# A two-block transformer kernel: five instead of six recombined pairs in each up-projection, with its row copies and turning sums spread out

## Chip, cores and metric

The kernel runs on one core of a Trainium2 chip. The metric is the device time of one execution in microseconds (us), less is better. TensorE (PE in the profile) multiplies, VectorE (DVE) and ScalarE (ACT) work on tiles in SBUF and on the PE's sums in PSUM, SyncE (SP) and GpSimd (POOL) issue DMAs. Each engine takes its own instructions in order, and semaphores order the engines against each other.

## The reference

The whole model is two blocks one after the other on a 512 x 1024 float32 activation. The part that matters here is the feed-forward of the first block, which runs twice (once a layer):

```
def conv_ffn(xn, w_up, conv_w, conv_b, w_down):
    h = causal_dwconv(xn @ w_up, conv_w) + conv_b
    gate, val = h[..., :FFN_DIM], h[..., FFN_DIM:]
    return (jax.nn.silu(gate) * val) @ w_down
...
for layer in range(DEPTH):                       # DEPTH = 2
    h = h + (gated_deltanet or chunk_attention)
    h = h + conv_ffn(rmsnorm(h, f_norm[layer]), f_w_up[layer], f_conv[layer], f_conv_b[layer], f_w_down[layer])
```

`w_up` is 1024 x 5632 (FFN_DIM is 2816, a gate half and a value half), and the convolution runs over three neighbouring rows of the sequence.

## The kernel before

**Precision.** Each float32 operand is used as two float32r parts, a rounded one (hi) and the rest (lo). A product is three matmuls: w_hi x_hi, w_hi x_lo and w_lo x_hi. A raw weight tile is loaded by SP into `wraw`, ACT copies it to hi (a cast, L1634 or L1952) and DVE makes lo by subtraction (L2351 or L2758), both in `wsplit`.

**The up-projection** (`ffn`, one function on each engine) works through KF = 22 pairs f = 0 to 21, each a gate tile and a value tile of 128 columns. Activations lie as 8 tiles of 128 x 512 (`xhi`, `xlo`). Pairs 0 and 1 are four tiles j = 0 to 3 in a loop of their own. Of the pairs from UP_FIRST = 2 on there are two kinds:

- A plain pair (`up_tile`, twice): 8 x 3 matmuls 128x512 for the gate into bank `pa`, the same for the value into bank `pb`, 48 in all.
- A block pair (`up_block`, for f in UP_BLOCKS): the 2 x 2 recombination of Strassen and Winograd, seven products in place of eight. It has seven forms (a11, s2, a12, s1, s3, s4, a22) of 4 x 3 matmuls 128x256, 84 in all. DVE builds s2 and s4 from weights (`sum_low`, `sum_high`), two POOL DMAs that add in flight build s1 and s3 out of the three quarter tiles of `load_bases`, and four forms (s2, s1, s3, a22) need turned activations xb1 to xb4.

**The turned activations** are made once a layer. ACT writes eight unsplit rows `x_raw` (L1998, step "raw"), DVE makes the four sums `turn` (L2777) into `xb_raw`, ACT casts them (`turn_hi`, L1977), and DVE subtracts (`turn_low`, L2781), in place over `xb_raw`. The matmuls of form s2 wait for `turn_low` 1, s1 for 0, s3 for 2 and a22 for 3.

**Weights roll** through a ring of six places in `wsplit`; a plain tile takes two places, a form one. The table UNITS_AFTER says which units are cast after which one is used: for plain pairs it is the unit three tiles on. `casts_after` on ACT and `lows_after` on DVE walk that table. The units after "old2" and "old3" are those that may overwrite the splits of tiles j = 2 and j = 3: the gate of pair 2, and the value of pair 2 with the gate of pair 3. Raw weights have one buffer for gates and one for values: SP issues `load_gate(f)` when `low` of the previous gate is done, then `load_value(f)`, then `load_bases(f+2)` where f + 2 is a block pair.

**Behind the matmuls.** For each pair DVE multiplies the bank by `rstd` (L2867, L2882, step "ev", which also frees the bank), ACT applies the newest tap (`newest`, L1968), DVE the two older ones (`conv`, L2763 and L2765), ACT the silu, DVE the product (L2896, step "hid"), and for f < UP_KEPT = 6 ACT and DVE split the row (`row_hi` L1983, `row_low` L2787). All steps of DVE and ACT are counted by two semaphores; `up_counts` lists them in the order of issue, and that list must agree with the engine code. So where a step stands in `up_counts` is where it stands in the engine's queue.

Before, block pairs are 4, 7, 10, 13, 16 and 19. All eight `x_raw` rows are written after tile j = 1, ahead of the casts for "old2". Sums 0 and 1 come between the gate and the value of pair 2, sums 2 and 3 after its value; their lows in the same places of pair 3.

Of the kernel before, what the change touches and what calls it, by code (L numbers as in the profile page):

```python
# [15 lines left out]
ALU = mybir.AluOpType  # L16
ACT = mybir.ActivationFunctionType
# [80 lines left out]


UP_FIRST = 2  # L100
UP_BLOCKS = (4, 7, 10, 13, 16, 19)
UP_FORMS = ("a11", "s2", "a12", "s1", "s3", "s4", "a22")
UP_KEPT = 6
UP_LOADS = (KF - UP_FIRST, KF - UP_FIRST - len(UP_BLOCKS), 3 * len(UP_BLOCKS), 0)
UP_SUMS = 32 * len(UP_BLOCKS)

# [36 lines left out]
def up_counts():  # L143

    def lows(q):
        return [("low", u) for u in UNITS_AFTER[q]]

    def his(q):
        return [("hi", u) for u in UNITS_AFTER[q]]

    dve = lows("old2") + lows("old3")
    act = [("raw", k) for k in range(KD)] + his("old2") + his("old3")
    for f in range(UP_FIRST, KF):
        if f in UP_BLOCKS:
            dve += lows((f, "a11")) + [("u", f)] + lows((f, "s2")) + [("c11", f)] + lows((f, "a12")) + [("w", f)] + lows((f, "s1"))
            dve += [("c22", f), ("v", f)] + lows((f, "s3")) + [("c12", f), ("ev", f, 0)] + lows((f, "s4")) + [("c21", f), ("ev", f, 1)]
            dve += lows((f, "a22")) + [("tap", f, 0), ("conv", f, 0), ("tap", f, 1), ("conv", f, 1), ("hid", f)]
            act += [("p", f)] + his((f, "a11")) + his((f, "s2")) + his((f, "a12")) + his((f, "s1")) + his((f, "s3")) + his((f, "s4"))
            act += [("newest", f, 0)] + his((f, "a22")) + [("newest", f, 1), ("silu", f)]
        else:  # L160
            dve += [("ev", f, 0)] + lows((f, "gate")) + [("tap", f, 0), ("conv", f, 0)]
            act += his((f, "gate")) + [("newest", f, 0)]
            if f + 1 in UP_BLOCKS:
                dve += [("s4", f + 1)]
            if f == UP_FIRST:
                dve += [("turn", 0), ("turn", 1)]
                act += [("turn_hi", 0), ("turn_hi", 1)]
            if f == UP_FIRST + 1:
                dve += [("turn_low", 0), ("turn_low", 1)]
            dve += [("ev", f, 1)]  # L170
            if f + 2 in UP_BLOCKS:
                dve += [("s2", f + 2)]
            dve += lows((f, "value")) + [("tap", f, 1), ("conv", f, 1), ("hid", f)]
            act += his((f, "value")) + [("newest", f, 1), ("silu", f)]
            if f == UP_FIRST:
                dve += [("turn", 2), ("turn", 3)]
                act += [("turn_hi", 2), ("turn_hi", 3)]
            if f == UP_FIRST + 1:
                dve += [("turn_low", 2), ("turn_low", 3)]
# [91 lines left out]
def build(nc, xT, w8, w11, w_gates, consts, vecs, a_log, dt_bias, rel_flip, ln_gb, w_spat, b_spat, outT,  # L271
# [5 lines left out]
    with ctx:  # L277
# [1349 lines left out]
        def _(act):  # L1627
# [299 lines left out]
            def ffn(layer, n, after, gain):  # L1927
# [57 lines left out]
                for j in range(4):  # L1985
                    f, g = j // 2, j % 2
                    cast_ahead(s, 0, j, True)
                    act.wait_ge(acc_free, s.number(0, j) + 1)
                    A(fy[:, j, :], tmp[:, j % 2, :], ACT.Identity, scale=w[:, g, f, 2:3], bias=wb[:, g, f, :]
                      ).then_inc(ev("ffn_newest"), 1)  # L1990
                    if g == 1:
                        act.wait_ge(ev("ffn_conv"), 4 * layer + j)
                        A(fy[:, j - 1, :], fy[:, j - 1, :], ACT.Silu).then_inc(ev("gate_silu"), 1)
                        act.wait_ge(ev("hid_ready"), f + (2 * layer + 1))
                        A(hid_hi[:, f, :], fy[:, j, :], ACT.Copy).then_inc(ev("hid_hi_ready"), 1)
                    if j == 1:
                        for k in range(KD):
                            A(x_raw[:, k, :], h[:, k, :], ACT.Copy, scale=xgain[:, k, :]).then_inc(ev("block_act"), 1)  # L1998
                    if j == 2:
                        casts_after("old2")  # L2000
                casts_after("old3")
                d = st[f"down{layer}"]
                for f in range(UP_FIRST, KF):
                    if f in UP_BLOCKS:
                        act.wait_ge(ev("form_used"), unit_used(layer, (f, "a11")))
                        if f != UP_BLOCKS[0]:
                            act.wait_ge(ev("block_dve"), UP_DVE[layer, "c11", UP_BLOCKS[UP_BLOCKS.index(f) - 1]])
                        A(unit_p, bank_1, ACT.Copy).then_inc(ev("block_act"), 1)
                        for name in UP_FORMS[:-1]:
                            casts_after((f, name))  # L2010
                        newest(f, 0)
                        casts_after((f, "a22"))
                        newest(f, 1)
                        gate_silu(f)
                    else:
                        casts_after((f, "gate"))
                        if f == KF - 1:
                            act.wait_ge(ev("form_used"), unit_used(layer, (f, "gate")))
                            cast(d, 0, 0)
                        newest(f, 0)  # L2020
                        if f == UP_FIRST:
                            turn_hi(0)
                            turn_hi(1)
                        casts_after((f, "value"))
                        newest(f, 1)
                        gate_silu(f)
                        if f == UP_FIRST:
                            turn_hi(2)
                            turn_hi(3)
                    if f < UP_KEPT:  # L2030
                        row_hi(f)
                    if f == KF - 2:
# [310 lines left out]
        def _(dve):  # L2343
# [403 lines left out]
            def ffn(layer, n, m_x, gain):  # L2747
# [22 lines left out]
                    else:  # L2770
                        dve.wait_ge(ev("ffn_conv"), 4 * layer + 3 + g)

                def turn(n, a, b, op):
                    dve.wait_ge(ev("block_act"), UP_ACT[layer, "raw", KD - 1])
                    if n in (1, 3):
                        dve.wait_ge(steps, UP_DVE[layer, "turn", 0 if n == 1 else 1])
                    tt_(xb_raw[n][:], a, b, op).then_inc(steps, 1)  # L2777
# [12 lines left out]
                for j in range(4):  # L2790
                    f, g = j // 2, j % 2
                    dve.wait_ge(acc_done, s.number(0, j) + 1)
                    tt_(tmp[:, j % 2, :], acc[:, j % 2, :], rstd[:], ALU.mult).then_inc(acc_free, 1)
                    low_ahead(s, 0, j, True)
                    dve.wait_ge(ev("ffn_newest"), 4 * layer + j + 1)
                    stt(fy[:, j, 1:S], tmp[:, j % 2, 0:S - 1], w[:, g, f, 1:2], fy[:, j, 1:S], ALU.mult, ALU.add
                        ).then_inc(ev("ffn_tap"), 1)
# [3 lines left out]
                    if g == 1:  # L2801
# [3 lines left out]
                        dve.wait_ge(ev("hid_hi_ready"), f + (2 * layer + 1))  # L2805
                        tt_(hid_lo[:, f, :], fy[:, j, :], hid_hi[:, f, :].bitcast(F32), ALU.subtract
                            ).then_inc(ev("hid_lo_ready"), 1)
                    if j == 2:
                        lows_after("old2")
                lows_after("old3")  # L2810
                d = st[f"down{layer}"]

                def used(f, name):
# [50 lines left out]
                def pair(f):  # L2864
# [6 lines left out]
                    conv(f, 0)  # L2871
                    if f + 1 in UP_BLOCKS:
                        sum_high(f + 1)
                    if f == UP_FIRST:
                        turn(0, x11r, x12r, ALU.subtract)
                        turn(1, xb_raw[0][:], x22r, ALU.add)
                    if f == UP_FIRST + 1:
                        turn_low(0)
                        turn_low(1)
                    used(f, "value")  # L2880
                    taken(f, 1)
                    tt_(tmp[:, 1, :], pb, rstd[:], ALU.mult).then_inc(steps, 1)  # L2882
# [5 lines left out]
                for f in range(UP_FIRST, KF):  # L2888
# [8 lines left out]
                    if f == UP_FIRST:  # L2897
                        turn(2, x12r, x22r, ALU.subtract)
                        turn(3, x21r, xb_raw[1][:], ALU.subtract)
                    if f == UP_FIRST + 1:  # L2900
                        turn_low(2)
                        turn_low(3)
# [587 lines left out]
```

## Time and profile before

| | |
|---|---|
| Median of 3 runs | 1779.31 us (1777.58 to 1780.95) |
| The profiled execution, its own time | 1780.4 us |
| Its span, first to last instruction | 1778.7 us |
| Mean granted TensorE clock | 0.993 of full speed |
| PE busy | 1727.2 us, 97% |
| DVE busy | 1260.4 us, 71% |
| ACT busy | 920.5 us, 52% |

A busy PE is one that has a matmul in flight. The matmuls of a stream overlap, so the time that one costs is the distance from its start to the start of the next, not its printed duration. The two up-projections lie at about 372 to 627 us (layer 0) and 1002 to 1258 us (layer 1) of the span. In the rows below, times are microseconds from the start of the span.

### The profile page before, as it was taken

How to read it: one execution, taken by the hardware profiler on the slowest of the kernel's cores; microseconds unless marked ns; L12 is line 12 of the kernel's file. 1: busy time of each engine (PE TensorE's matmuls, PEld its weight loads, DVE VectorE, ACT ScalarE, POOL GpSimd, SP SyncE). 2: the span in 40 equal slices, each digit the busy share in tenths (PEclk: the TensorE clock that was granted, in tenths of full speed). 3: DMA queues.
4: the chain of work that ended last, by engine and by line, in shares of the span. 5: the costliest groups of instructions: out<-in, count | busy, mean ns of one | idle time of the engine just before them, and what ended most of it. 6: DMA issues, size and time to landing. Idle time of an engine off the chain costs nothing.

```text
span 1778.7 us, 26360 instructions
## 1 busy us (share of the span) xinstructions
PE 1727.2 (97%) x9776; PEld 1385.3 (78%) x9776; DVE 1260.4 (71%) x2148; ACT 920.5 (52%) x1509; POOL 72.0 (4%) x109
## 2 busy tenths in 40 slices
PE   9999999998999999999999979999999999999998
PEld 6777777776888878788887768888788766678987
DVE  6788888568888853467776687888633567677875
ACT  5656666454444442368776544444522456654442
POOL 2000000000000000000000000000000000101100
PEclk9999999999999999999999999999999999999999
DMA  5522221133345322243331324343321311325632
GB/s 184 180 77 72 72 72 48 48 114 102 99 122 146 118 93 98 72 118 106 106 106 63 101 77 136 89 144 109 120 98 63 100 48 60 101 93 138 156 110 68
DMA packets 56799, 178.99 MB, mean 101 GB/s; under 512 B 7041, under 2 KB 9364, under 8 KB 56688
## 3 DMA queue, kind: packets, MB, share of 16 engines
q1 hardware_dynamic: 46320, 152.98, 25.9%
q0 software_dynamic: 9936, 24.43, 6.4%
q8 instruction: 73, 1.20, 0.3%
q14 instruction: 38, 0.31, 0.1%
q10 hardware_dynamic: 432, 0.07, 0.0%
HBM read 170.83 MB, written 6.63 MB: 100 GB/s over the span
## 4 chain that ended last, share of the span: by engine, by line
PE 78%; DVE 10%; ACT 5%; issue 5%; DMA 2%; POOL 0%; DVEq 0%; SPq 0%; ACTq 0%; POOLq 0%
PE acc L943 11%; PE acc L945 10%; PE acc L944 10%; PE acc L969 8%; PE pa L1265 3%; PE pbc L1267 3%; PE pa L1267 3%; PE pbc L1265 3%; PE pbc L1266 3%; PE pa L1266 3%; DMA wraw<-w 1%; DVE wsplit L2758 1%; DVE wsplit L2351 1%; ACT wsplit L1634 1%; PE acc L1293 1%
## 5 line engine op out<-in xcount | busy, mean ns | idle before, releaser
L1634 ACT ACTIVATE wsplit<-wraw 128x1024 fp32r<-128x1024 f32 (+1 forms) x149 | 167.0, 1124 | 226.3 <-PE acc L945 207.1
L2351 DVE TENSOR_TENSOR wsplit<-wraw,wsplit 128x1024 fp32r<-128x1024 f32 (+1 forms) x146 | 191.0, 1310 | 113.9 <-ACT wsplit L1634 112.5
L1952 ACT ACTIVATE wsplit<-wraw 128x512 fp32r<-128x512 f32 (+1 forms) x140 | 109.5, 798 | 165.2 <-DMA wraw<-w 40.4
L943 PE MATMUL acc<-xhi,wsplit 128*128 128x512 f32 x448 | 189.5, 423 | 1.0 <-DVE at_vs L2939 1.0
L945 PE MATMUL acc<-xhi,wsplit 128*128 128x512 f32 x448 | 177.9, 397 | 0.0
L944 PE MATMUL acc<-xlo,wsplit 128*128 128x512 f32 x448 | 177.6, 396 | 0.0
L969 PE MATMUL acc<-xhi,wsplit 128*128 128x512 f32 x464 | 158.2, 413 | 0.1
L2758 DVE TENSOR_TENSOR wsplit<-wraw,wsplit 128x512 fp32r<-128x512 f32 (+1 forms) x140 | 123.8, 901 | 36.5 <-ACT wsplit L1952 36.3
L943 PE MATMUL acc<-hid_hi,wsplit 128*128 128x512 f32 x352 | 139.9, 397 | 2.0 <-DVE wsplit L2351 1.4
L945 PE MATMUL acc<-hid_hi,wsplit 128*128 128x512 f32 x352 | 139.6, 396 | 0.0
L944 PE MATMUL acc<-hid_lo,wsplit 128*128 128x512 f32 x352 | 139.5, 396 | 0.0
L943 PEld LDWEIGHTS acc<-xhi,wsplit 128*128 128x128 f32 x448 | 84.5, 189 | 33.5 <-issue 13.8
L1265 PE MATMUL pa<-xhi,wsplit 128*128 128x512 f32 x224 | 90.3, 403 | 10.7 <-DVE wsplit L2758 9.7
L945 PEld LDWEIGHTS acc<-xhi,wsplit 128*128 128x128 f32 x448 | 84.4, 188 | 20.2
L969 PE MATMUL acc<-xlo,wsplit 128*128 128x512 f32 x232 | 99.1, 427 | 0.0
L944 PEld LDWEIGHTS acc<-xlo,wsplit 128*128 128x128 f32 x448 | 84.9, 189 | 17.0 <-issue 1.4
L969 PEld LDWEIGHTS acc<-xhi,wsplit 128*128 128x128 f32 x464 | 83.7, 189 | 17.2 <-issue 1.9
L1265 PE MATMUL pbc<-xhi,wsplit 128*128 128x512 f32 x224 | 88.9, 397 | 0.9 <-DVE wsplit L2758 0.9
L1267 PE MATMUL pa<-xhi,wsplit 128*128 128x512 f32 x224 | 89.5, 399 | 0.0
L1266 PE MATMUL pa<-xlo,wsplit 128*128 128x512 f32 x224 | 89.3, 399 | 0.0
L1267 PE MATMUL pbc<-xhi,wsplit 128*128 128x512 f32 x224 | 88.8, 396 | 0.0
L1266 PE MATMUL pbc<-xlo,wsplit 128*128 128x512 f32 x224 | 88.8, 396 | 0.0
(563 smaller groups left out, 4214.0 us busy)
## 6 DMA issues: line engine op xcount, KB each, us to landing
wraw<-w SPq DMA_DIRECT2D x201, 512.0 KB, 3.8
wraw<-w SPq DMA_DIRECT2D x32, 704.0 KB, 4.1
wraw<-w SPq DMA_DIRECT2D x57, 256.0 KB, 3.4
wraw<-w POOLq DMA_DIRECT2D x38, 256.0 KB, 5.5
bias_dram<-ext_dram POOLq DMA_DIRECT2D x1, 4096.0 KB, 21.4
bias<-bias_dram POOLq DMA_DIRECT2D x16, 256.0 KB, 3.0
at_ks<-at_ks SPq DMA_DIRECT2D x16, 256.0 KB, 2.9
crow<-row_dram POOLq DMA_DIRECT2D x8, 256.0 KB, 3.7
```

Of the source, the lines that this page charges most:

```text
L943: mm(out, whi[:, k, :], a[:, x_at + k, :], start=(k == first), stop=False)
L944: mm(out, whi[:, k, :], b[:, x_at + k, :], start=False, stop=False)
L945: m = mm(out, wlo[:, k, :], a[:, x_at + k, :], start=False, stop=(k == last))
L969: d = mm(bank(s, i, j), w[:, k, :], x[:, k, :], start=(m == 0), stop=(m == 3 * KD - 1))
L1265: mm(out, whi[:, k, :], xhi[:, k, :], start=(k == 0), stop=False)
L1266: mm(out, whi[:, k, :], xlo[:, k, :], start=False, stop=False)
L1267: m = mm(out, wlo[:, k, :], xhi[:, k, :], start=False, stop=(k == KD - 1))
L1293: mm(out, whi[:, k, :], x[1][:, k, :], start=False, stop=False)
L1634: A(split(s, i, j, 0), raw(s, j), ACT.Copy).then_inc(w_hi_ready, 1)
L1952: A(unit_split(u, 0), unit_raw(u), ACT.Copy).then_inc(ev("block_act"), 1)
L2351: tt_(split(s, i, j, 1), raw(s, j), split(s, i, j, 0).bitcast(F32), ALU.subtract).then_inc(w_lo_ready, 1)
L2758: tt_(unit_split(u, 1), unit_raw(u), unit_split(u, 0).bitcast(F32), ALU.subtract).then_inc(steps, 1)
```

## The change

UP_BLOCKS loses its first entry, 4, so pair 4 becomes a plain pair. Pairs 2 to 6 are then five plain pairs in a row, and pair 7 is the first block. The table of the ring (`up_units`) follows by itself. ACT writes two `x_raw` rows after each of the tiles j = 0 to 3. The units after "old2" and "old3" are cast and lowered inside iterations j = 2 and j = 3, ahead of the newest tap of that tile. The four turning sums are issued singly: sum 0 between gate and value of pair 2, sum 1 after its value, sums 2 and 3 likewise in pair 3; each is cast one half pair later (the last in pair 4's second half), and the lows come in 4 first half, 4 second half, 5 first half and 6 second half.

```diff
-UP_BLOCKS = (4, 7, 10, 13, 16, 19)
+UP_BLOCKS = (7, 10, 13, 16, 19)
+TURNS = {(2, 0): (0,), (2, 1): (1,), (3, 0): (2,), (3, 1): (3,)}
+TURN_HIS = {(2, 1): (0,), (3, 0): (1,), (3, 1): (2,), (4, 1): (3,)}
+TURN_LOWS = {(4, 0): (0,), (4, 1): (1,), (5, 0): (2,), (6, 1): (3,)}
...
     # ACT, ffn, for j in range(4)
                     cast_ahead(s, 0, j, True)
+                    if j >= 2:
+                        casts_after(("old2", "old3")[j - 2])
...
-                    if j == 1:
-                        for k in range(KD):
-                            A(x_raw[:, k, :], h[:, k, :], ACT.Copy, scale=xgain[:, k, :]).then_inc(ev("block_act"), 1)
-                    if j == 2:
-                        casts_after("old2")
-                casts_after("old3")
+                    for k in (2 * j, 2 * j + 1):
+                        A(x_raw[:, k, :], h[:, k, :], ACT.Copy, scale=xgain[:, k, :]).then_inc(ev("block_act"), 1)
...
-                        if f == UP_FIRST:
-                            turn_hi(0)
-                            turn_hi(1)
+                        for k in TURN_HIS.get((f, 0), ()):
+                            turn_hi(k)
...
-                        if f == UP_FIRST:
-                            turn_hi(2)
-                            turn_hi(3)
+                        for k in TURN_HIS.get((f, 1), ()):
+                            turn_hi(k)
...
     # DVE, ffn, for j in range(4)
                     low_ahead(s, 0, j, True)
+                    if j >= 2:
+                        lows_after(("old2", "old3")[j - 2])
...
-                    if j == 2:
-                        lows_after("old2")
-                lows_after("old3")
...
     # DVE, pair(f), first half; the second half likewise after the pair's product
-                    if f == UP_FIRST:
-                        turn(0, x11r, x12r, ALU.subtract)
-                        turn(1, xb_raw[0][:], x22r, ALU.add)
-                    if f == UP_FIRST + 1:
-                        turn_low(0)
-                        turn_low(1)
+                    for k in TURNS.get((f, 0), ()):
+                        turn(k)
+                    for k in TURN_LOWS.get((f, 0), ()):
+                        turn_low(k)
```

`up_counts` is changed in the same way.

## Rows read from the trace of the kernel before

**Rows 1.** The page, part 1: busy time, share of span, instructions.
```profile
PE 1727.2 (97%) x9776; PEld 1385.3 (78%) x9776; DVE 1260.4 (71%) x2148; ACT 920.5 (52%) x1509; POOL 72.0 (4%) x109
```

**Rows 2.** Stretches: length, busy us (instructions) of PE, PEld, DVE, ACT, POOL, clock, DMA.
```profile
389.60:459.40 69.80, 58.66 (x277) 48.70 (x277) 57.65 (x78) 31.89 (x44) 1.72 (x2) 0.93 0.29 83
...
392.30:396.30 4.00, 3.94 (x12) 3.16 (x13) 2.80 (x5) 1.42 (x3) 0.00 (x0) 0.67 0.41 135
...
424.90:427.70 2.80, 2.73 (x13) 2.76 (x14) 2.77 (x5) 1.34 (x2) 0.00 (x0) 0.50 0.60 243
...
1055.20:1059.30 4.10, 4.06 (x19) 4.09 (x20) 3.96 (x7) 1.46 (x3) 0.00 (x0) 0.50 0.41 164
```

**Rows 3.** Timeline of PE, layer 0: start, us, instruction, idle before it.
```profile
389.33 0.39 PE L945 MATMUL acc<-xhi,wsplit 128*128 128x512 f32 x1
392.36 0.50 PE L1265 MATMUL pa<-xhi,wsplit 128*128 128x512 f32 x1 [2.64 <-DVE wsplit L2758]
...
399.61 0.40 PE L1265 MATMUL pbc<-xhi,wsplit 128*128 128x512 f32 x1
...
405.23 0.40 PE L1265 MATMUL pa<-xhi,wsplit 128*128 128x512 f32 x1
...
416.48 0.28 PE L1292 MATMUL acc<-xhi,wsplit 128*128 128x256 f32 x1
...
417.77 0.28 PE L1294 MATMUL acc<-xhi,wsplit 128*128 128x256 f32 x1
...
424.97 0.55 PE L1292 MATMUL acc<-xb_hi,wsplit 128*128 128x256 f32 x1 [6.92 <-DVE xb_lo L2781]
...
436.48 0.50 PE L1265 MATMUL pa<-xhi,wsplit 128*128 128x512 f32 x1 [1.45 <-DVE wsplit L2758]
...
459.42 0.28 PE L1292 MATMUL acc<-xhi,wsplit 128*128 128x256 f32 x1
...
469.27 0.28 PE L1294 MATMUL acc<-xb_hi,wsplit 128*128 128x256 f32 x1
...
470.54 0.50 PE L1265 MATMUL pa<-xhi,wsplit 128*128 128x512 f32 x1 [0.99 <-DVE wsplit L2758]
```

**Rows 4.** Timeline of PE, layer 1.
```profile
1019.68 0.39 PE L945 MATMUL acc<-xhi,wsplit 128*128 128x512 f32 x1
...
1055.24 0.55 PE L1292 MATMUL acc<-xb_hi,wsplit 128*128 128x256 f32 x1 [7.22 <-DVE xb_lo L2781]
...
1090.53 0.28 PE L1292 MATMUL acc<-xhi,wsplit 128*128 128x256 f32 x1
```

**Rows 5.** Timeline of ACT, layer 0.
```profile
383.35 0.63 ACT L1995 ACTIVATE hid_hi<-fy 128x512 fp32r<-128x512 f32 x1 [2.04 <-DVE fy L2804]
383.89 5.00 ACT L1998 ACTIVATE x_raw<-h,vec 128x512 f32<-128x512 f32 x8
388.80 0.80 ACT L1989 ACTIVATE fy<-tmp,vec 128x512 f32<-128x512 f32 x1
389.50 1.04 ACT L1952 ACTIVATE wsplit<-wraw 128x1024 fp32r<-128x1024 f32 x1
...
402.65 1.06 ACT L1952 ACTIVATE wsplit<-wraw 128x1024 fp32r<-128x1024 f32 x1 [3.89 <-DMA wraw<-w]
```

**Rows 6.** Timeline of DVE, layer 0.
```profile
391.09 1.22 DVE L2758 TENSOR_TENSOR wsplit<-wraw,wsplit 128x1024 fp32r<-128x1024 f32 x1
...
404.88 0.75 DVE L2763 SCALAR_TENSOR_TENSOR fy<-tmp,vec,fy 128x511 f32<-128x511 f32 x1
...
406.33 1.22 DVE L2777 TENSOR_TENSOR xb_raw<-x_raw 128x1024 f32<-128x1024 f32 x1
...
422.47 2.35 DVE L2781 TENSOR_TENSOR xb_lo<-xb_raw,xb_hi 128x1024 fp32r<-128x1024 f32 x2
424.74 0.68 DVE L2882 TENSOR_TENSOR tmp<-pbc,rstd 128x512 f32<-128x512 f32 x1
```

**Rows 7.** Timeline of SP's DMA issues, layer 0: `load_value(3)`.
```profile
399.09 0.33 SPq L735 DMA_DIRECT2D wraw<-w  x1
```

More of the change, by code:

```diff
@@ L151, in up_counts @@
     dve = lows("old2") + lows("old3")
-    act = [("raw", k) for k in range(KD)] + his("old2") + his("old3")
+    act = [("raw", k) for k in range(4)] + his("old2") + [("raw", 4), ("raw", 5)] + his("old3") + [("raw", 6), ("raw", 7)]
     for f in range(UP_FIRST, KF):
@@ L164, in up_counts @@
                 dve += [("s4", f + 1)]
-            if f == UP_FIRST:
-                dve += [("turn", 0), ("turn", 1)]
-                act += [("turn_hi", 0), ("turn_hi", 1)]
-            if f == UP_FIRST + 1:
-                dve += [("turn_low", 0), ("turn_low", 1)]
+            dve += [("turn", k) for k in TURNS.get((f, 0), ())] + [("turn_low", k) for k in TURN_LOWS.get((f, 0), ())]
+            act += [("turn_hi", k) for k in TURN_HIS.get((f, 0), ())]
             dve += [("ev", f, 1)]
@@ L174, in up_counts @@
             act += his((f, "value")) + [("newest", f, 1), ("silu", f)]
-            if f == UP_FIRST:
[L176 to L179, printed above, removed]
+            dve += [("turn", k) for k in TURNS.get((f, 1), ())] + [("turn_low", k) for k in TURN_LOWS.get((f, 1), ())]
+            act += [("turn_hi", k) for k in TURN_HIS.get((f, 1), ())]
         if f < UP_KEPT:
@@ L2026, in ffn @@
                         gate_silu(f)
-                        if f == UP_FIRST:
-                            turn_hi(2)
-                            turn_hi(3)
+                        for k in TURN_HIS.get((f, 1), ()):
+                            turn_hi(k)
                     if f < UP_KEPT:
@@ L2771, in taken, with turn @@
                         dve.wait_ge(ev("ffn_conv"), 4 * layer + 3 + g)
-                def turn(n, a, b, op):
+                def turn(n):
+                    a, b, op = ((x11r, x12r, ALU.subtract), (xb_raw[0][:], x22r, ALU.add),
+                                (x12r, x22r, ALU.subtract), (x21r, xb_raw[1][:], ALU.subtract))[n]
                     dve.wait_ge(ev("block_act"), UP_ACT[layer, "raw", KD - 1])
@@ L2873, in pair @@
                         sum_high(f + 1)
-                    if f == UP_FIRST:
-                        turn(0, x11r, x12r, ALU.subtract)
-                        turn(1, xb_raw[0][:], x22r, ALU.add)
-                    if f == UP_FIRST + 1:
-                        turn_low(0)
-                        turn_low(1)
+                    for k in TURNS.get((f, 0), ()):
+                        turn(k)
+                    for k in TURN_LOWS.get((f, 0), ()):
+                        turn_low(k)
                     used(f, "value")
@@ L2896, in ffn @@
                     tt_(y if f < UP_KEPT else hid_raw[:, f, :], y, fy[:, f % 2 * 2, :], ALU.mult).then_inc(steps, 1)
[L2897 to L2902, printed above, removed]
+                    for k in TURNS.get((f, 1), ()):
+                        turn(k)
+                    for k in TURN_LOWS.get((f, 1), ()):
+                        turn_low(k)
                     if f < UP_KEPT:
```

## The prediction, made before the changed kernel was run

> **What bounds the kernel now.** I read the page first, then the stretches around the change, then the timelines of PE, ACT, DVE and SP there. The page gives PE 97% of the span [rows 1], so time can be won only by giving PE less work or by closing its gaps. The stretch from the last tile of pairs 0 and 1 to the first matmul of pair 7 is where the change acts: of 69.8 us PE is busy 58.7, at a mean clock of 0.93 [rows 2]. This is far from the 97%, and the same stretch comes again in layer 1.
>
> The timeline of PE says where that goes. Tile j = 3 issues its last matmul at 389.33. One 128x512 matmul costs 0.2345 us in a stream: the 24 of the value of pair 2 run from 399.61 to 405.23, the 48 of pair 3 from 405.23 to 416.48 [rows 3]. So PE could go on at 389.56. What follows, in layer 0 [rows 3]:
> - PE waits until 392.36 for the lo part of the first weights of pair 2, 2.80 us.
> - The gate of pair 2 then takes 392.36 to 399.61, 7.25 us where 5.63 would do, 1.62 too much. This is a slow clock (0.67 granted in its first 4 us [rows 2]) and a short wait.
> - Form a11 of pair 4 issues its last matmul at 417.77, and s2 starts at 424.97: 7.08 us lost to `turn_low` 1.
> - The twelve matmuls of s2 run at the lower clock level, 1.2 GHz, granted 0.50 [rows 2].
> - The next pair starts at 436.48. From 416.48 it is 20.0 us for block 4. Block 7 takes 459.42 to 469.39, 9.97 us for 84 matmuls (0.1187 each). So block 4 costs 10.03 more than a block without stalls, the 7.08 and the slow clock among it.
> - From 436.48 to 459.42 are pairs 5 and 6, 22.94 us, of which 22.51 is matmuls: 0.43 lost.
>
> Check: 2.80 + 1.62 + 10.03 + 0.43 = 14.88 us of loss; matmuls 4 x 11.255 + 9.97 = 54.99; sum 69.87, and 459.42 - 389.56 = 69.86.
>
> Layer 1 has the same shape: from 1019.91 (the last matmul of tile 3 starts at 1019.68) to 1090.53 it is 70.62 us [rows 4], so 15.63 of loss. Form s2 waits 7.22 us there [rows 4], and 4.1 us from its start on are granted 0.50 [rows 2].
>
> **The change part by part.**
>
> PE work. Pair 4 goes from 84 half-width matmuls, 9.97 us, to 48 full ones, 11.26 us: 1.29 us more a layer, certain, on the bound engine. PE gets 72 instructions fewer in all, which by itself gives nothing. At one place I set a rule against the row: the trace has 0.2345 and 0.1187 us per matmul. The Trainium skill, "TensorE: Matmul & The Clock Gate", section "Back-to-back issue gap", gives 518 and 262 cycles for 512 and 256 columns, 0.2158 and 0.1092 us at 2.4 GHz. By that the extra work would be 10.36 - 9.17 = 1.19 us, and five pairs would be an estimated 51.8 us instead of 56.3. The trace disagrees with the page by 9% for these instructions, and the sum goes by the trace.
>
> The first gate. Before, ACT writes eight `x_raw` rows (5.00 us, 0.62 each) from 383.89, then the newest tap at 388.80, and only then the first cast for pair 2 at 389.50; the low follows from 391.09 for 1.22, and PE starts [rows 3, 5, 6]. Now ACT has written rows 0 and 1 after tile 0, and after `hid_hi` (383.35) only rows 2 and 3, until about 385.15. Then comes the cast, because it now stands ahead of the newest tap: 385.15 to 386.2. DVE is idle there, low until about 387.5. PE needs it at 389.56: slack 2.1 us, the wait of 2.80 goes. The first two rows cost tile 0's queue 1.25 us; they end near 378.5, where the next cast began anyway, and tile 3 whose weights that is starts at 384. Cover gone, this costs at most 1.25 in a place with 3 us to spare.
>
> What the early low sets off. SP waits for it to issue `load_gate(3)`, now near 387.5. A load takes 399.09 to 402.65 = 3.56 us to the cast that waits for it [rows 5, 7], so it lands near 391.1. ACT casts pair 2's value at 389.6 to 390.6, and then stands waiting for gate 3 until 391.1. Queued behind are the newest tap of tile 3, its silu, `hid_hi` and rows 6 and 7, and DVE's two older taps wait for them. Newest tap 3 ends near 392.9, and DVE ends the row product of pair 1 near 397.0, `x_raw` near 397.5. PE needs the value of pair 2 at 395.2 (low done about 392.1) and gate 3 at 400.8 (about 393.4): nothing late.
>
> Five pairs in a row. DVE's costs are 0.68 for a bank times rstd, 0.75 a tap, 1.22 a low or a sum, 2.35 for two turned lows [rows 6]. Back to back a pair is 2 x 0.6 + 2 x 1.15 + 4 x 0.78 + 0.6 + 0.6 = 7.8 us; five are 39, four sums and four turned lows 9.5, `sum_low` and `sum_high` for pair 7 some 1.3: 50 us in the 56.3 that PE needs. No engine becomes the bound, but the order decides. I walked it with PE's tiles ending at 395.2, 400.8, 406.4, 412.1, 417.7, 423.3, 429.0, 434.6, 440.2, 445.8:
> - Pair 2: bank gate 397.0 to 397.7, low of value 3 to 399.8, taps, sum 0 to 402.5, bank value to 403.1, low of gate 4 to 404.3, taps, product, sum 1 to 407.8, row to 408.5.
> - Pair 3: bank gate to 409.1, low of value 4 to 410.3, taps, sum 2 to 413.0, bank value to 413.6, low of gate 5 to 414.8, taps, product, sum 3 to 418.2, row to 418.9.
> - Pair 4: bank gate to 419.5, low of value 5 to 420.7; here DVE catches up: turned low 0 to 423.4, bank value to 424.3, turned low 1 to 429.4. Pair 5: turned low 2 near 434.5. Pair 6: turned low 3 near 451.4.
>
> Against that PE wants: gate 3's bank (freed 397.7) at 400.8, value 3's (403.1) at 406.4, gate 4's (409.1) at 412.1, value 4's (413.6) at 417.7; the weights of value 3 (399.8) at 406.4, gate 4 (404.3) at 412.1, value 4 (410.3) at 417.7. The smallest slack is 3.0 us. Block 7 starts at 445.8 and wants turned low 1 at once and the last one at 454.3, 2.9 us after it is done. Each low frees a raw buffer and the load lands 3.56 later, 7 us or more ahead of its cast. The bases of pair 7 are issued after `load_value(5)`, near 411, POOL's adding DMAs after them; DVE wants them at 435. SP drops three quarter loads of pair 4 and gets one value load, POOL drops two DMAs; none of them was waited for.
>
> After block 7 starts. UNITS_AFTER from pair 5 on is the same list as before, the ring meets pair 7 in the same place. The only difference is the turned low 3 ahead of block 7's steps, 1.2 us on a DVE that before waited twice in that block; the 1.27 us after it (469.27 to 470.54 [rows 3]) stay, since that wait hangs on the end of form s4. I take 0 for it, bounds 0 and +1.2 a layer. The lower bound of everything: all losses gone, that is what I take. The upper: one to three of the slacks above fail by a few us.
>
> Sum. Layer 0: 69.86 - 56.28 = 13.6 us. Layer 1: 70.62 - 56.28 = 14.3 us. Together 27.9. The profiled execution took 1780.4 with a span of 1778.7; it becomes 1752.5 and 1750.8. The median of the runs is 1.1 below the profiled one: 1751.4.
>
> **The rivals.**
> - R1, DVE runs late in the five pairs. It has only 6 us spare of 56, and each sum stands ahead of a bank that PE waits for. For it: before, PE did wait on DVE after block 4 (1.45 idle [rows 3]). Against: 3 us of slack at the tightest. If the slack is eaten in pairs 3 and 4, 1 to 5 us a layer come back, more if the clock falls too: 1754 to 1762, middle 1757.
> - R2, the stall moves to pair 7: the turned lows are still late when PE gets there, so that the saving does not come for this part. Then 7.08 + 1.1 us of slow clock stay in layer 0 and as much or more in layer 1: 1751.4 + 16.5 = 1768. Against: they are due at 429.4 and wanted at 447.
> - R3, slower. The last turned low, placed after pair 6's product, holds form a22 of pair 7, and PE stands still. It would have to end 13.6 us after 454.3 to eat the whole gain, at 468, where I have 451.4. With 15 us more than that in both layers the time would be 1783. Even if all eight turning steps, 9.5 us, lay bare on PE the gain would be 4 us a layer. No row supports it.
> - R4, the page's shorter gap between matmuls: five pairs in 51.8 us in place of 56.3 would give 9 us more, 1742.5. The rows of the same instructions speak against it.
>
> **How the numbers follow.** All stalls gone: 0.75. R1 0.16, R2 0.05, R3 0.015, R4 0.01, the rest 0.015 for something unseen that leaves the time as it is. The likeliest gives 1751.4. A measurement tells 0.2%, 3.6 us, from nothing. Range: down to 1748, for run to run spread (the three runs span 3.4 us) and other small waits that shift; up to 1758, which takes in 1.2 a layer at block 7 and the nearer half of R1. Faster by over 0.2%: 0.96, same 0.02, slower 0.02.
>
> **What would show it.** PE from tile j = 3 to form a11 of pair 7 without an idle entry of over 0.3 us and at clock 1.00, 56.3 us long in both layers; the first cast for pair 2 near 385; the sum singly between the halves; bank and low of pair 3 and 4 done 3 us before PE asks; block 7 to pair 8 again near 11.1 us. I am wrong if PE waits for a rstd product (a bank) in pairs 3 or 4, if s2 or a22 of pair 7 waits on a turned low, or if a gap appears further on that was not there.

## The result and the profile after

The changed kernel takes 1751.62 us (median of 6 runs, 1751.03 to 1754.15), the one before 1778.99 us (6 runs) in the same session. The ratio is 0.9847, 95% interval 0.9835 to 0.986. That is 27.4 us less; the prediction said 27.9 less and 1751.4 us.

The page of the changed kernel: span, part 1 (busy time, share of span, instructions), and part 4 (shares of the chain that ended last).

```profile
span 1752.5 us, 26132 instructions
...
PE 1723.7 (98%) x9704; PEld 1380.3 (79%) x9704; DVE 1248.0 (71%) x2120; ACT 914.7 (52%) x1497; POOL 68.6 (4%) x105
...
PE 86%; DVE 6%; ACT 4%; issue 3%; DMA 1%; POOL 0%; SPq 0%; DVEq 0%; ACTq 0%
```

PE has only 72 instructions and 3.5 us of busy time less than before [rows 1], while the span fell by 26.2 us. So the gain is closed gaps, not less work. The stretches say where they were (columns as in [rows 2]). The first two run from tile j = 3 to form a11 of pair 7, one a layer; the third runs from there to the gate of pair 9, in layer 0.

```profile
389.90:446.20 56.30, 56.30 (x243) 45.24 (x241) 49.44 (x62) 30.05 (x39) 1.78 (x2) 1.00 0.33 101
...
1006.20:1062.50 56.30, 56.30 (x242) 45.23 (x242) 49.44 (x62) 30.05 (x39) 1.77 (x2) 1.00 0.32 102
...
446.20:468.60 22.40, 21.39 (x134) 18.88 (x132) 17.58 (x27) 9.53 (x14) 1.72 (x2) 1.00 0.57 177
```

Where 69.8 us held 58.7 of busy PE at a clock of 0.93 [rows 2], now 56.3 us hold 56.3 at 1.00. DVE needs 49.4 us of them; the walk had said 50. The timeline of PE gives the ends (start, us, instruction, idle before it), layer 0 and then layer 1:

```profile
389.74 0.40 PE L942 MATMUL acc<-xhi,wsplit 128*128 128x512 f32 x1
389.97 0.39 PE L1262 MATMUL pa<-xhi,wsplit 128*128 128x512 f32 x1
...
412.46 0.40 PE L1262 MATMUL pa<-xhi,wsplit 128*128 128x512 f32 x1
...
446.20 0.28 PE L1289 MATMUL acc<-xhi,wsplit 128*128 128x256 f32 x1
...
455.94 0.28 PE L1291 MATMUL acc<-xb_hi,wsplit 128*128 128x256 f32 x1
457.22 0.50 PE L1262 MATMUL pa<-xhi,wsplit 128*128 128x512 f32 x1 [1.01 <-DVE wsplit L2751]
...
1006.26 0.39 PE L1262 MATMUL pa<-xhi,wsplit 128*128 128x512 f32 x1
...
1062.48 0.28 PE L1289 MATMUL acc<-xhi,wsplit 128*128 128x256 f32 x1
```

From 389.97 to 446.20 it is 56.23 us, from 1006.26 to 1062.48 it is 56.22; the prediction had 56.28 for both. Against the 69.86 and 70.62 of before that is 13.63 and 14.40 us. No idle entry of PE lies in either. Pair 8 starts 11.02 us after block 7 does, behind the same 1.0 us wait as before [rows 3], where 11.12 stood.

The engines behind it, in layer 0: ACT, DVE and SP.

```profile
384.29 1.32 ACT L1996 ACTIVATE x_raw<-h,vec 128x512 f32<-128x512 f32 x2
385.51 1.04 ACT L1949 ACTIVATE wsplit<-wraw 128x1024 fp32r<-128x1024 f32 x1
```

```profile
386.59 1.23 DVE L2751 TENSOR_TENSOR wsplit<-wraw,wsplit 128x1024 fp32r<-128x1024 f32 x1 [0.88 <-ACT wsplit L1949]
...
408.24 0.68 DVE L2861 TENSOR_TENSOR tmp<-pa,rstd 128x512 f32<-128x512 f32 x1
...
450.55 1.22 DVE L2776 TENSOR_TENSOR xb_lo<-xb_raw,xb_hi 128x1024 fp32r<-128x1024 f32 x1
```

```profile
387.85 0.33 SPq L729 DMA_DIRECT2D wraw<-w  x1
```

Two `x_raw` rows stand ahead of the first cast instead of eight [rows 5]; it starts at 385.51 (walk: 385.15) and its low ends at 387.82, 2.2 us before PE wants it. The bank of pair 3's gate is free at 408.92 (walk: 409.1), and PE wants it at 412.46 for the gate of pair 4: 3.5 us of slack. The last turned low ends at 451.77 (walk: 451.4). SP issues the gate load of pair 3 at 387.85.

The two stretches give 28.0 us, yet the two spans differ by 26.2. PE's waits in the profile after show the rest (us in total, times, longest): 1.9 us on `yb_lo`, in the merge near 1585, far behind the up-projections, which end at about 1230. The kernel before has no such wait.

```profile
PE pa L940 <- DVE yb_lo L3130: 1.9, 1, 1.9
```

DVE makes `yb_lo` behind a sum of weights, and that sum waits for the second of two adding DMAs that POOL issues (`sums_landed`). POOL and DVE there, first in the kernel before, then in the changed one:

```profile
1602.34 1.20 POOL L927 DMA_DIRECT2D wraw<-w  x1
...
1602.79 0.68 DVE L3115 TENSOR_TENSOR gz<-gu,gz 128x512 f32<-128x512 f32 x1
...
1607.88 0.69 DVE L3191 TENSOR_TENSOR wraw<-wraw 128x512 f32<-128x512 f32 x1 [4.41 <-issue]
```

```profile
1574.84 1.18 POOL L924 DMA_DIRECT2D wraw<-w  x1
...
1574.85 0.68 DVE L3105 TENSOR_TENSOR gz<-gu,gz 128x512 f32<-128x512 f32 x1
...
1581.69 0.69 DVE L3181 TENSOR_TENSOR wraw<-wraw 128x512 f32<-128x512 f32 x1 [6.16 <-issue]
```

The size of this wait differs between executions of one kernel, but whether it is there follows the block list. All eleven profiled executions with five blocks have it: 1.9, 1.2 and 1.2 us in the changed kernel (here, e4, e13), 1.7 in e1, 0.8 in e2, 0.5 in e5, 0.9 in e6, 1.8 in e7, 1.2 in e10, 0.9 in e11, 0.8 in e14. None of the three with six blocks has it (before, e3, e9). DVE stands 4.8 to 6.2 us ahead of its sum with five blocks and 3.8 to 4.4 with six. With six, POOL issues the DMA 0.45 to 1.24 us ahead of DVE's product `gz`; with five, from 0.07 ahead of it to 0.45 behind. So this wait counts as a cost of the change. How a block less in the up-projection moves POOL's issue in the merge was not tried, and stays open.

### The profile page after: what moved, and what is told of

Read it like the earlier page. It is cut to its first block, busy times and chain, and to the rows that moved or that the text cites. A ratio compares the mean times of both kernels' runs of the same rounds, so it can differ in the third digit from the quotient of the medians.

```text
span 1752.5 us, 26132 instructions
## 1 busy us (share of the span) xinstructions
PE 1723.7 (98%) x9704; PEld 1380.3 (79%) x9704; DVE 1248.0 (71%) x2120; ACT 914.7 (52%) x1497; POOL 68.6 (4%) x105
## 4 chain that ended last, share of the span: by engine, by line
PE 86%; DVE 6%; ACT 4%; issue 3%; DMA 1%; POOL 0%; SPq 0%; DVEq 0%; ACTq 0%
PE acc L940 12%; PE acc L941 11%; PE acc L942 11%; PE acc L966 9%; PE pa L1262 3%; PE pbc L1264 3%; PE pa L1264 3%; PE pbc L1262 3%; PE pbc L1263 3%; PE pa L1263 3%; ACT wsplit L1631 1%; PE acc L1291 1%; PE acc L1290 1%; PE acc L1289 1%; PE pbc L1453 1%
## 5 line engine op out<-in xcount | busy, mean ns | idle before, releaser
L1949 ACT ACTIVATE wsplit<-wraw 128x512 fp32r<-128x512 f32 (+1 forms) x130 | 105.4, 825 | 165.5 <-PE pbc L1264 62.7
L2751 DVE TENSOR_TENSOR wsplit<-wraw,wsplit 128x512 fp32r<-128x512 f32 (+1 forms) x130 | 119.6, 934 | 32.5 <-ACT wsplit L1949 32.3
L940 PEld LDWEIGHTS acc<-xhi,wsplit 128*128 128x128 f32 x448 | 84.3, 188 | 33.4 <-issue 13.8
L1262 PE MATMUL pa<-xhi,wsplit 128*128 128x512 f32 x240 | 95.4, 398 | 2.0 <-DVE wsplit L2751 2.0
L1262 PE MATMUL pbc<-xhi,wsplit 128*128 128x512 f32 x240 | 95.2, 397 | 0.0
L1264 PE MATMUL pa<-xhi,wsplit 128*128 128x512 f32 x240 | 95.2, 396 | 0.0
L1264 PE MATMUL pbc<-xhi,wsplit 128*128 128x512 f32 x240 | 95.1, 396 | 0.0
L1263 PE MATMUL pbc<-xlo,wsplit 128*128 128x512 f32 x240 | 95.1, 396 | 0.0
L1263 PE MATMUL pa<-xlo,wsplit 128*128 128x512 f32 x240 | 95.1, 396 | 0.0
```

The source lines that it names most:

```text
L940: mm(out, whi[:, k, :], a[:, x_at + k, :], start=(k == first), stop=False)
L1262: mm(out, whi[:, k, :], xhi[:, k, :], start=(k == 0), stop=False)
L1263: mm(out, whi[:, k, :], xlo[:, k, :], start=False, stop=False)
L1264: m = mm(out, wlo[:, k, :], xhi[:, k, :], start=False, stop=(k == KD - 1))
L1949: A(unit_split(u, 0), unit_raw(u), ACT.Copy).then_inc(ev("block_act"), 1)
L2751: tt_(unit_split(u, 1), unit_raw(u), unit_split(u, 0).bitcast(F32), ALU.subtract).then_inc(steps, 1)
```

## The experiments

Twelve runs. Every time is a median, and each ratio is to the kernel before on the same chip (1779.47, 1780.78, 1777.39 and 1779.85 us in the four groups: e1 to e4; e5, e6, e7, e9; e10, e11; e13, e14).

My theory: each part of the change does one thing in each layer. The first-gate wait goes by spreading the rows and by casting early. The s2 wait goes by starting blocks at 7. No new wait comes, because singly issued sums leave 3 us of slack. The rival: DVE has so much to spare that the order of the sums is worth nothing, or the parts simply add up.

### e1: the block list alone

```
# the kernel before, with
-UP_BLOCKS = (4, 7, 10, 13, 16, 19)
+UP_BLOCKS = (7, 10, 13, 16, 19)
```

> The kernel before with block pair 4 made a plain pair, and nothing else: eight x rows in one go after tile 1, casts of pair 2 behind the newest taps, turning sums in twos in pairs 2 and 3. Theory: the order of the row copies and sums carries about as much as the removed block. The first gate waits its 2.8 us, the slow clock or the next wait costs 1.0 to 1.6, and DVE, held up by the sums in twos, frees the gate bank of pair 3 only near 419.3, so PE stands about 2.9 us at pair 4 and about 1.4 at pair 5: 8.4 us a layer of the 13.6 and 14.3 come back, 1768 us (1763 to 1771). Rival: the block at pair 4 was the whole cost, and the spreading is hidden anyway: only the 2.8 and 1.6 stay, 1757 to 1760.

1774.41 us (1772.23 to 1775.94), ratio 0.9966 [0.9956, 0.9977]: 5 us faster, not 11. The stretches are 64.90 and 65.72 us long, 8.7 and 9.5 more than in the changed kernel, as expected. In layer 0, beside the first-gate wait (2.63) and two short ones (0.87 at the value of pair 2, 0.82 at the gate of pair 5), PE's timeline has these two:

```profile
417.47 0.48 PE L1265 MATMUL pa<-xhi,wsplit 128*128 128x512 f32 x1 [3.37 <-DVE tmp L2867]
...
477.10 0.66 PE L1265 MATMUL pa<-xhi,wsplit 128*128 128x512 f32 x1 [2.12 <-DVE tmp L2867]
```

The first is the gate of pair 4 waiting for its bank: with five plain pairs in a row and the sums two at a time DVE is late. The second, at the gate of pair 9, lies outside the stretch, and I had not expected it; layer 1 has it too (2.05). What stands behind it is on ACT:

```profile
470.34 1.06 ACT L1952 ACTIVATE wsplit<-wraw 128x1024 fp32r<-128x1024 f32 x1 [6.30 <-DMA wraw<-w]
```

ACT stood 6.30 us for the raw weights of gate 9 with the newest tap of pair 7 queued behind, and DVE, which needs that tap, freed the bank late. This is what I had left out in the prediction too, and e7 and e10 go after it.

### e2: the changed kernel with its sums two at a time

```
-TURNS = {(2, 0): (0,), (2, 1): (1,), (3, 0): (2,), (3, 1): (3,)}
-TURN_HIS = {(2, 1): (0,), (3, 0): (1,), (3, 1): (2,), (4, 1): (3,)}
-TURN_LOWS = {(4, 0): (0,), (4, 1): (1,), (5, 0): (2,), (6, 1): (3,)}
+TURNS = {(2, 0): (0, 1), (2, 1): (2, 3)}
+TURN_HIS = {(2, 0): (0, 1), (2, 1): (2, 3)}
+TURN_LOWS = {(3, 0): (0, 1), (3, 1): (2, 3)}
```

The edit puts the casts and the turned lows back to their old places too (casts in the same half pair, lows in pair 3), so it tests the whole order of the turning steps and not the pairing of the sums by itself.

> The changed kernel with the turning sums issued in twos in pair 2 and their lows in twos in pair 3, as before. Theory: DVE and ACT come late by one extra step in each half pair, the bank of gate 3 is freed about 1 us after PE wants it, and small waits of 0.7 to 1.0 us follow at value 3 and gate 4: 2.6 us a layer, 1756 us (1754 to 1759). Rival: the 3 us of slack cover it, 1751.6 (within 1).

1764.09 us (1761.06 to 1765.78), ratio 0.9909 [0.9888, 0.993]. That is 13.0 us above the changed kernel of the same chip (e4), where 5 were expected. The profiled execution is the fastest of the four, 3.0 us under the median. In its stretches it loses 3.98 and 3.5 us. The chain in layer 0, on ACT, DVE and PE:

```profile
408.03 2.19 ACT L1974 ACTIVATE xb_hi<-xb_raw 128x1024 fp32r<-128x1024 f32 x2 [3.44 <-DVE xb_raw L2772]
...
410.78 0.69 DVE L2782 TENSOR_TENSOR hid_lo<-fy,hid_hi 128x512 fp32r<-128x512 f32 x1 [1.64 <-ACT hid_hi L1980]
411.39 0.68 DVE L2861 TENSOR_TENSOR tmp<-pa,rstd 128x512 f32<-128x512 f32 x1
...
412.22 0.47 PE L1262 MATMUL pa<-xhi,wsplit 128*128 128x512 f32 x1 [2.21 <-DVE tmp L2861]
```

The cost is not the length of the sums on DVE alone. ACT casts both turned tiles (2.19 us) ahead of `hid_hi` of pair 2, DVE waits 1.64 us for that row, and the bank, free at 408.92 in the changed kernel, is free at 412.07. The other part is gate 9 again: in layer 0 its load was issued at 458.65 and its cast began at 466.25, 7.6 us, and PE waited 2.83 us. In layer 1 there is no such wait.

### e3: rows and early casts alone

The changed kernel with six block pairs from 4 on, and the sums as in e2.

```
-UP_BLOCKS = (7, 10, 13, 16, 19)
+UP_BLOCKS = (4, 7, 10, 13, 16, 19)
 # TURNS, TURN_HIS and TURN_LOWS as in e2
```

> The kernel before, six blocks and sums in twos, but with the x rows written two a tile and the casts of pair 2 ahead of the newest taps. Theory: the first gate's wait and the slow clock after it go (4.4 us), and form s2 of pair 4 starts as soon as turned low 1 is there, near 418.9 in place of 424.8, so its wait shrinks from 7.1 to about 5.4: 5.9 us a layer gained, 1767 us (1763 to 1770). Rival: turned low 1 is not earlier, since the chain through it does not pass the rows, and the saved wait comes back at s2: 1777 to 1779.

1774.83 us (1771.7 to 1780.4), ratio 0.9973 [0.996, 0.9986]: 5 us faster, not 12. The first gate no longer waits, but s2, where [rows 3] has 6.92, waits longer:

```profile
420.26 0.55 PE L1289 MATMUL acc<-xb_hi,wsplit 128*128 128x256 f32 x1 [8.06 <-DVE xb_lo L2776]
```

In layer 1 it is 7.58 where it was 7.22. I had expected 5.4 us; that was wrong. `turn_low` 1 does end earlier, 33.4 us behind the end of tile j = 3 in layer 0 where it was 35.3, but PE gains more than that. Of the 4.4 us won at the first gate in layer 0, 1.1 are lost again at s2 and 1.4 in pairs 2 and 3, so that the stretch is 1.9 us shorter. In layer 1, where little is lost again, it is 4.3 us shorter. The profiled execution, 2.7 us under the median, shows more of a gain than the median does.

### e11: blocks and single sums, rows and casts as before

The third pair of parts: `x_raw` in one go after tile 1 and the first casts behind the newest tap, as in the kernel before, the rest changed.

```
-    act = [("raw", k) for k in range(4)] + his("old2") + [("raw", 4), ("raw", 5)] + his("old3") + [("raw", 6), ("raw", 7)]
+    act = [("raw", k) for k in range(KD)] + his("old2") + his("old3")
...
-                    if j >= 2:
-                        casts_after(("old2", "old3")[j - 2])
...
-                    for k in (2 * j, 2 * j + 1):
-                        A(x_raw[:, k, :], h[:, k, :], ACT.Copy, scale=xgain[:, k, :]).then_inc(ev("block_act"), 1)
+                    if j == 1:
+                        for k in range(KD):
+                            A(x_raw[:, k, :], h[:, k, :], ACT.Copy, scale=xgain[:, k, :]).then_inc(ev("block_act"), 1)
+                    if j == 2:
+                        casts_after("old2")
+                casts_after("old3")
 # lows_after on DVE likewise
```

> The changed kernel with the rows as before: eight x rows in one go after tile 1, casts of pair 2 behind the newest taps; five blocks and single sums stay. Theory: only the first gate's wait (2.8 us) and what follows it in pair 2 (1.0 to 1.6) come back, since with single sums the bank of gate 3 is freed 2.2 us before PE wants it: 4.1 us a layer, 1760 us (1758.5 to 1763). Rival: the late loads of pairs 2 and 3 hold DVE so that further waits follow at pairs 3 and 4, 1765 or more.

1760.43 us (1759.41 to 1760.76), ratio 0.9892 [0.9861, 0.9924], as expected. Its stretches lose 5.66 and 4.0 us, all at pair 2. In layer 0 that is the 2.62 below and a slow clock behind it (24 matmuls of the gate in 8.5 us), in layer 1 it is 2.62 and 0.87.

```profile
390.10 0.80 PE L1262 MATMUL pa<-xhi,wsplit 128*128 128x512 f32 x1 [2.62 <-DVE wsplit L2753]
```

Spread rows and early casts were not run apart. ACT's rows only suggest their shares: two rows (1.32 us) in place of eight (5.00) ahead of the cast give it 3.7 us, going ahead of the newest tap (0.80) gives 0.7.

### e4 and e13: the changed kernel again

Unedited, on the chips of e1 to e3 and of e14.

> The changed kernel once more, nothing edited. Its profile showed one wait that the kernel before did not have, 1.9 us on yb_lo at the start of the merge stage, 1100 us behind the change in the program. Theory: that is the landing time of DMAs, different from execution to execution, and not of the change: here it lies between 0 and 2 us again, and the time is 1751.6 (within 1.5). Rival: it comes from the change, and shows as 1.9 us again.

> The changed kernel, unedited, on the same chip as the next one. Theory: 1751.5 (within 1.5).

1751.12 us (1750.85 to 1752.18), ratio 0.9835 [0.9815, 0.9855], and 1751.47 us (1749.91 to 1753.18), ratio 0.983 [0.9811, 0.9849]. The wait on `yb_lo` is 1.2 us in both; e4's theory, that it is not of the change, does not hold against all the profiles (above).

### e5 and e6: how much slack there is

More DVE work at the one place where the walk was tightest: 2 or 5 sums of 128x1024 at the end of pair 2, read from raw tiles and written to a part of `wraw` that nothing reads at that time.

```
+PADS = 2          # e6: 5
...
+            dve += [("pad", k) for k in range(PADS if f == UP_FIRST else 0)]
...
+                    for k in range(PADS if f == UP_FIRST else 0):
+                        if k:
+                            dve.wait_ge(steps, UP_DVE[layer, "pad", k - 1])
+                        tt_(wraw[:, 4096:5120].rearrange("p (k n) -> p k n", n=HALF), x12r, x22r, ALU.subtract).then_inc(steps, 1)
```

> The changed kernel with two more VectorE sums of 128x1024, written to an unused stretch and read by nobody, at the end of pair 2. Theory: in the profile of the changed kernel the gate bank of pair 3 is freed at 408.93 and PE comes for it at 412.46, so DVE has 3.5 us to spare there and more at all later places. Two sums cost 2.5 us: no PE wait, 1751.5 (within 1.5). Rival: DVE has no real spare time (50 of 56 us), what is added appears at PE: 2.5 us a layer, 1756.5.

> The same with five more sums, 6.2 us. Theory: 6.2 - 3.5 = 2.7 us of PE wait at the gate of pair 4, and up to 1.6 us of slow clock behind it as in the kernels with a wait of 2.2 to 3.4 there: 2.7 to 4.4 us a layer, 1757 to 1760.5. Rival: all of it shows, 6.2 us a layer, 1764.

e5: 1752.12 us (1750.36 to 1754.19), ratio 0.9832 [0.9817, 0.9847], and no idle entry of PE in the stretch; its two sums take 2.48 us. e6: 1758.42 us (1757.34 to 1759.2), ratio 0.987 [0.9855, 0.9885]. Five sums take 6.26 us of DVE's queue, and PE's time from pair 2 to pair 4 grows by 2.78 us in both layers. 6.26 - 2.78 = 3.48, and the slack read from the changed kernel is 412.46 - 408.92 = 3.54. DVE and PE of e6:

```profile
405.16 6.26 DVE L2898 TENSOR_TENSOR wraw<-x_raw 128x1024 f32<-128x1024 f32 x5
...
412.76 0.47 PE L1264 MATMUL pa<-xhi,wsplit 128*128 128x512 f32 x1 [2.62 <-DVE tmp L2863]
```

The stretches behind this wait, layer 0 and layer 1, columns as in [rows 2]:

```profile
412.70:418.50 5.80, 5.74 (x25) 4.67 (x26) 5.76 (x7) 4.20 (x6) 0.00 (x0) 1.00 0.61 203
1032.20:1039.40 7.20, 7.17 (x24) 5.75 (x25) 7.03 (x9) 4.92 (x6) 0.00 (x0) 0.76 0.67 214
```

The same wait is followed by a gate at clock 1.00 in one layer and at 0.76 in the other, some 1.5 us dearer.

### e7, e14 and e10: the unused places of the ring

The ring must close after a multiple of six places. With five blocks two places are over, and `up_units` gives them to form a22 of pair 7 (4 instead of 2). So gate 8 may be cast only when form s4 of block 7 has been used (ACT at 454.85, idle for 5.28 us), and SP, which waits for its low, issues gate 9 at 457.20. With the places elsewhere the table casts gate 8 behind form s1, two forms earlier. e7 gives the two places to the value of pair 4, where all units are cast well ahead.

```
-    spread = UP_BLOCKS[:(-places) % RING // 2]
+    spread = ((4, "value"),)
...
         if f not in UP_BLOCKS:
-            return 2
-        return 1 if name != "a22" else 4 if f in spread else 2
+            return 4 if (f, name) in spread else 2
+        return 1 if name != "a22" else 2
```

> The changed kernel with the two unused places of the weight ring moved from form a22 of pair 7 to the value tile of pair 4. With them in the block, the gate of pair 8 is cast only after form s4, and PE waits 1.01 us for it (3.98 us from s4 to pair 8 where later blocks need 2.82), and the gate of pair 9 is cast ahead of pair 7's newest tap, so a late DMA of it holds ACT and DVE: 0.1 to 3 us at pair 9 in the profiles so far. Theory: both go, 1.16 us and some tenths a layer, and nothing comes instead, as the casts at pair 4 have more than 3 us to spare: 1749.0 (1748.3 to 1750). Rival: the gate of pair 6, cast early, waits for its DMA at pair 4's value and holds the chain there, 1751.5 to 1755.

1748.46 us (1748.17 to 1749.62), ratio 0.9816 [0.9802, 0.9829]. From a11 of pair 7 to the gate of pair 9 it is 21.1 us in both layers, without an idle entry, where the changed kernel has 22.37 (above) and 22.56. That is 2.7 us in all. Layer 0 of e7:

```profile
444.10:465.20 21.10, 21.10 (x133) 18.90 (x132) 18.93 (x28) 10.40 (x14) 1.72 (x2) 1.00 0.64 188
```

SP issues gate 9 and ACT casts it, first in e7, then in the changed kernel:

```profile
452.41 0.33 SPq L729 DMA_DIRECT2D wraw<-w  x1
...
456.76 1.06 ACT L1949 ACTIVATE wsplit<-wraw 128x1024 fp32r<-128x1024 f32 x1 [1.80 <-DMA wraw<-w]
```

```profile
457.20 0.33 SPq L729 DMA_DIRECT2D wraw<-w  x1
...
461.77 1.06 ACT L1949 ACTIVATE wsplit<-wraw 128x1024 fp32r<-128x1024 f32 x1 [3.97 <-DMA wraw<-w]
```

e14 is that kernel again, on one chip with e13.

> The kernel with the unused places of the ring at the value tile of pair 4, beside the changed kernel. Theory: PE's stretch from pair 7's first form to pair 9 was 21.10 us in both layers against 22.37 and 22.56, so it is 2.7 us faster than its neighbour: 1748.7 (within 1). Rival: the difference seen so far was between chips, and both lie within 0.5 us.

1748.07 us (1746.82 to 1749.32), ratio 0.9814 [0.9795, 0.9834]: 3.4 us below e13, and no run of one lies among those of the other. So this version beats both kernels. The two stretches explain 2.7 of the 3.4.

e10 is e2 with the same edit, to tell whether the wait at pair 9 came from there.

> The kernel with the sums in twos (1764.1 us, where I had expected 1756) and the two unused places of the ring moved to the value tile of pair 4. Theory: the waits in pairs 2 to 6 account for 3.7 us a layer of its loss, and the rest of the 12.5 us is the DMA of gate 9, which lands late behind the loads for pair 10 and is cast ahead of pair 7's newest tap (2.8 us of PE wait in one layer of its profile). With the gap moved that goes: 1748.5 + 7.4 = 1756 (1754 to 1757.5). Rival: the sums in twos cost more than the waits in their stretch show, 1760 or more.

1756.44 us (1755.94 to 1757.44), ratio 0.9871 [0.9839, 0.9902]. The wait at pair 9 is gone. What stays are 2.20 us at the gate of pair 4 in both layers, and at the gate of pair 5 a wait for weights of 1.71 in layer 0 and 0.17 in layer 1. Against e7 and e14 (1748.46 and 1748.07) the old order of the turning steps costs 8 us, and e10's stretches are 4.4 us longer in each layer than theirs. These runs are of different chips: taken against the kernel before of its own chip the cost is 11 us (21.0 gained against 32.3 and 31.8). So of e2's 13 us 2 to 5 need the ring as it was, and e2's profile shows 2.83 of them, at pair 9.

### e9: six blocks, from pair 5 on

```
-UP_BLOCKS = (7, 10, 13, 16, 19)
+UP_BLOCKS = (5, 8, 11, 14, 17, 20)
...
+TURN_HIS = {(2, 1): (0,), (3, 0): (1,), (3, 1): (2,), (4, 0): (3,)}
+TURN_LOWS = {(4, 0): (0, 1), (4, 1): (2, 3)}
```

> The changed kernel with six blocks again, at pairs 5, 8, 11, 14, 17 and 20; turning sums as in the change, all their lows in pair 4. PE work is that of the kernel before, 1.29 us less a layer. Theory: with three plain pairs ahead DVE has 33.8 us for some 36 us of work; form s2 of pair 5 waits 1 to 3 us for turned low 1, and the ring has two blocks with unused places, 1.16 us more each layer: 1753 to 1759. Rival: the waits stay hidden and six blocks win, 1749.

1758.83 us (1757.8 to 1761.05), ratio 0.9871 [0.9856, 0.9886]. The sixth block saves 1.29 us of matmuls a layer, but PE waits again, in both layers: 0.47 at s2, 0.67 at s3, and at the gate of pair 6

```profile
436.19 0.50 PE L1262 MATMUL pa<-xhi,wsplit 128*128 128x512 f32 x1 [1.82 <-DVE wsplit L2751]
```

with a slow clock behind it (0.76 granted over the next 7.2 us), and 1.0 at pair 9. It loses 7 us to the changed kernel (1751.12 to 1751.62). A block at pair 5 meets turned lows and weights that are not ready.

## Why the prediction was right

- **PE work.** Predicted +1.29 us a layer, at 0.2345 and 0.1187 us a matmul. The stretch is 240 full matmuls in 56.23 us, 0.2343 each. R4 would have made it 51.8 us. The Trainium skill's gap for 512 columns, which it gives for an isolated matmul ("TensorE: Matmul & The Clock Gate", "Back-to-back issue gap"), is 0.2158 us; the trace disagrees in this kernel too.
- **The first gate.** Predicted 2.80 and 1.62 us to vanish, slack 2.1. Both are gone, slack 2.2. e11 shows that the rows and casts together do this: without them 5.7 and 4.0 us come back.
- **Five pairs in a row.** Predicted smallest slack 3.0 us, at the bank for the gate of pair 4; read 3.54, and measured by e5 (2.5 us more of DVE work is free) and e6 (6.26 us costs 2.78).
- **s2 and the slow clock.** Predicted 7.08 us and the time at 1.2 GHz to vanish. The forms of block 7 run without a wait for a turned low, all at 1.00. R2 is out in both layers.
- **Block 7 to pair 8.** Predicted 0, bounds 0 and +1.2; measured -0.1.
- **R1** did not happen, but was near. The bank it named is the one that waits in e1 (3.37), e2 (2.21) and e6 (2.62). Its price, 1 to 5 us a layer, holds for e2's stretches (3.98, 3.5) and about for e1's: of the 8.7 and 9.5 us there, 4.7 and 5.1 lie between the gate of pair 3 and pair 7, the rest is the first gate and what follows it.
- **R3** did not happen: the last turned low ends at 451.77, and form a22 starts at 454.65. Its price of 1783 us does not come out of its own terms: 15 us in each layer on top of 1751.4 are 1781.4.

The sum was 0.5 us off in the total (27.9 for 27.4) and 0.1 in each stretch. It lacks one term, the 1.9 us on `yb_lo`: the profiled execution was forecast at 1752.5 us and took 1754.15. By the prediction's own list this is a sign of being wrong, a gap further on that was not there before; it is small, and does not touch the mechanism. That the median came within 0.2 us of 1751.4 is partly luck. The profiled execution lies 2.5 us over its median, where 1.1 was taken, and that made up for the missing term. Executions differ by more than that: in the eleven profiles in which the first gate of pair 2 waits for nothing, it starts anywhere from 386.8 to 391.0 us.

Two things the prediction did not have. First, the parts do not add. Against the kernel before on their own chips blocks alone bring 5.1 us, rows alone 4.6, blocks with rows 15.4, blocks with single sums 17.0, and all three 28. Single sums alone, and rows with single sums on six blocks, were not run. What the traces show of the reason: every stall sits in front of the next, and a PE that comes earlier runs into a DVE that is earlier by less (8.06 for 6.92 in e3), or, without block 4, into a bank that DVE has not yet freed (3.37 in e1). Second, I read "the ring meets pair 7 in the same place" as no risk, but the cast of gate 9 stands ahead of pair 7's newest tap and depends on a load issued late. It cost PE no wait in the changed kernel's profile, where 4.6 us passed from issue to cast, and 2.1 us in both layers of e1 and 2.8 in layer 0 of e2, where 6.8 to 7.6 us passed. In e1, e2 and e3 my expectations failed at this or at the size of the wait that follows. The times expected for e5, e6, e7, e9, e10 and e11, made after these traces, held, though e9's main wait came at the gate of pair 6 and not at s2.

What stays open: what makes the load of gate 9 land late (the last section has what goes along with it), and how the block list sets the `yb_lo` wait. Neither was isolated.

## What to carry to other kernels

Write down, for each hand-over (a bank, a weight tile, a raw buffer), when it is ready and when it is wanted; the smallest difference says how much work may be put in, and here it held to 0.1 us. Small pieces between hand-overs beat the same work in lumps, above all where a second engine's lump (here two casts) stands ahead of something the first one waits for. Look through each in-order queue for an instruction that waits on a DMA with urgent work behind it: moving two idle ring places to where nothing was late gave 3.4 us more at no cost in work.

## What the runs showed of the hardware

- After one and the same wait of PE the clock fell in one layer and not in the other. In e2, 2.21 us at the gate of pair 4 in both; then in layer 0 and layer 1:

```profile
412.20:419.40 7.20, 7.18 (x24) 5.74 (x25) 7.13 (x9) 3.01 (x4) 0.00 (x0) 0.76 0.55 182
...
1035.60:1041.40 5.80, 5.72 (x25) 4.65 (x26) 5.77 (x7) 2.12 (x3) 0.00 (x0) 1.00 0.63 193
```

  Each stretch is one gate of 24 matmuls. A clock of 0.76 is a mean of the two levels, 1.2 and 2.4 GHz. So a wait of some 2.2 to 2.6 us costs its own length or 1.5 us more, and which of the two can't be read from the wait. In e9 the wait of 1.82 us at pair 6 was followed by 0.76 in both layers.
- Two loads of equal size, gate 9 in the changed kernel and in e2, took 4.6 and 7.6 us from issue to the cast that waited for them. What goes along with it is whether POOL's adding DMAs were issued just before. In layer 0 of e2 the first of them goes out 1.41 us ahead of the load:

```profile
457.24 0.84 POOL L872 DMA_DIRECT2D wraw<-w  x1 [35.82 <-DMA wraw<-w]
...
458.65 0.33 SPq L729 DMA_DIRECT2D wraw<-w  x1
...
466.25 1.06 ACT L1949 ACTIVATE wsplit<-wraw 128x1024 fp32r<-128x1024 f32 x1 [7.00 <-DMA wraw<-w]
```

  In the changed kernel it goes out at 457.25, 0.05 us behind the load. In all twelve loads of gate 9 in the profiles of the changed kernel (three), e5, e6 and e11, the two issues lie within 0.4 us of each other, and the load lands 4.5 to 4.8 us after its issue. In e1 and e2 the adding DMA is 1.1 to 1.4 us ahead: three of these four loads land after 6.7, 6.8 and 7.5 us, one after 4.5. No run set this order on purpose, so it is not shown to be the cause.
